# Seven of sixteen experts on slots of 64 tokens, in plain fp32 on two column tiles of TensorE

## What is computed

```python
scores = sigmoid(h @ w_router)
sel = scores + b_router
...  # best of 4 groups of 4 experts, then the top 2 experts in it
combine = sum(one_hot(idx, 16) * wts[..., None], axis=1)
for e in range(16):
    y_e = (silu(h @ w1[e]) * (h @ w3[e])) @ w2[e]      # 1024 -> 512 -> 1024
    y = y + combine[:, e:e + 1] * y_e
```

## Time and profile before

| | |
|---|---|
| median of 3 runs | 941.02 us |
| lowest and highest | 938.82, 943.4 us |
| the profiled execution: span from first to last instruction | 937.8 us |
| TensorE, VectorE, ScalarE, POOL busy over the span | 88%, 67%, 55%, 24% |
| read from HBM, written | 190.64 MB, 23.10 MB |
| granted TensorE clock, mean | 0.960 of full |

### The profile page before, as it was taken

One profiled execution on the slowest core, in us unless ns is written; L12 is line 12 of the kernel. 1 busy time (PEld: TensorE's weight loads), 2 busy tenths in 40 slices (PEclk: granted clock), 3 DMA queues, 4 the chain that ended last, 5 costly groups with the idle time before them and its releaser, 6 DMA issues. The chain is left out here.

```text
span 937.8 us, 15876 instructions
## 1 busy us (share of the span) xinstructions
PE 822.2 (88%) x6374; PEld 696.5 (74%) x6374; DVE 625.2 (67%) x804; ACT 515.8 (55%) x814; POOL 222.9 (24%) x336
## 2 busy tenths in 40 slices
PE   4998997999889998798769789849999999999990
PEld 2677866889669886598659788737888888888870
DVE  1596764458553685345455457487999998999965
ACT  3575742457424663237433344357877777777751
POOL 3114161123301252013400110016232222321112
PEclk9999999999989999899989999959999999999996
DMA  9977468245862369437685238807999999999934
GB/s 313 280 244 191 123 167 214 67 111 143 183 178 80 102 155 228 104 84 257 192 200 169 83 116 289 329 10 254 344 363 385 380 378 383 388 373 374 380 144 156
DMA packets 220053, 209.00 MB, mean 223 GB/s; under 512 B 51101, under 2 KB 156230, under 8 KB 219338
## 3 DMA queue, kind: packets, MB, share of 16 engines
q1 hardware_dynamic: 217241, 203.80, 68.9%
q0 software_dynamic: 2736, 4.15, 1.3%
HBM read 190.64 MB, written 23.10 MB: 228 GB/s over the span
## 5 line engine op out<-in xcount | busy, mean ns | idle before, releaser
L2061 DVE TENSOR_TENSOR w_lo<-raw,w_hi 128x2048 fp32r<-128x2048 f32 x96 | 233.4, 2450 | 23.1 <-ACT w_hi L1496 22.1
L2282 PE MATMUL bank<-hT,half_hi 128*128 128x256 f32 (+1 forms) x1024 | 229.8, 320 | 11.5 <-DVE half_lo L1616 5.3
L1496 ACT CAST w_hi<-raw 128x2048 fp32r<-128x2048 f32 x96 | 183.2, 1912 | 41.1 <-PE bank L2282 39.5
L2282 PEld LDWEIGHTS bank<-hT,half_hi 128*128 128x128 f32 x1024 | 168.3, 194 | 27.8 <-issue 9.3
L2282 PE MATMUL bank<-hT,half_lo 128*128 128x256 f32 (+1 forms) x512 | 160.2, 313 | 0.0
L2282 PE MATMUL bank<-w_hi,window 128*128 128x512 f32 x480 | 156.8, 398 | 0.0
L1616 DVE TENSOR_TENSOR half_lo<-half_raw,half_hi 128x1024 fp32r<-128x1024 f32 x88 | 108.7, 1237 | 55.5 <-ACT half_hi L1056 55.0
L2282 PE MATMUL bank<-lane 64*64 64x64 f32 (+2 forms) x2096 | 101.9, 237 | 19.4 <-issue 8.0
L2282 PEld LDWEIGHTS bank<-lane 64*64 64x64 f32 (+2 forms) x2096 | 93.4, 149 | 30.9 <-issue 15.6
L1056 ACT CAST half_hi<-half_raw 128x1024 fp32r<-128x1024 f32 x88 | 92.1, 1048 | 25.7 <-PE bank L2282 9.2
L2282 PEld LDWEIGHTS bank<-w_hi,window 128*128 128x128 f32 x480 | 90.4, 188 | 20.5
(11 more groups left out here) (321 smaller groups left out, 1272.3 us busy)
## 6 DMA issues: line engine op xcount, KB each, us to landing
raw<-in_w_e_dram SPq DMA_DIRECT2D x96, 1024.0 KB, 8.6
half_raw<-in_w_in_dram SPq DMA_DIRECT2D x64, 512.0 KB, 5.1
half_raw<-in_w_ada_dram SPq DMA_DIRECT2D x32, 512.0 KB, 4.9
raw<-in_w_ada_dram SPq DMA_DIRECT2D x8, 1024.0 KB, 11.3
dense<-staged SPq DMA_DIRECT2D x32, 128.0 KB, 4.5
half_raw<-in_w_proj_a_dram SPq DMA_DIRECT2D x8, 512.0 KB, 5.4
half_raw<-in_w_proj_b_dram SPq DMA_DIRECT2D x8, 512.0 KB, 4.1
half_raw<-in_w_out_dram SPq DMA_DIRECT2D x8, 512.0 KB, 8.0
```

The source lines that it names most:

```text
L1496: act.copy(e_hi[n % WBUF][:, :], slots[n % SLOTS_AHEAD][:, :]).then_inc(s["hi_ready"], 1)
L2061: dve.tensor_tensor(e_lo[n % WBUF][:, :], slots[n % SLOTS_AHEAD][:, :], e_hi[n % WBUF][:, :].bitcast(F32), ALU.subtract)\
L2282: return nc.tensor.matmul(dst, lhsT, rhs, start=start, stop=stop)
```

## The change

**Ranking.** Experts 0 and 1 stay in their places. The other fourteen are ranked on the chip by their number of tokens (`rank_loads`, `order_experts` on VectorE), and places 2 to 15 of the stream take them in a fixed pattern: ranks 1 to 7 go to wide places of 128 rows, ranks 8 to 14 to narrow places of 64. There are 512 rows, so rank 8 has at most 512 / 8 = 64. The pattern is `WIDTH`: places 0, 1, 3, 5, 7, 9, 11, 13 and 14 are wide, places 2, 4, 6, 8, 10, 12 and 15 narrow. SP reads an expert's number from `order_int` into a register before its first load.

**Narrow experts.** Their weights are not split: the product is plain fp32, straight from the slot of the ring, so the slot is freed by TensorE (`unit_used`) and not by VectorE. The window is hi + lo, [128, 8, 64]. The output has 64 rows, so the array is used as two tiles of 64 columns: in `narrow_up` the tiles take the two halves of a chunk's 512 columns, in `narrow_down` the two halves of the output's 1024, with both down units at once. Activations are [128, 256], turned in two pieces and copied once (`narrow_act`); the output needs one copy (`narrow_copy`) in place of two.

**Bookkeeping.** POOL's set-up writes the tables for it (some 30 small operations more). `place_rows` counts the expert of the last place, and not number 15, as the last. The last place's store is two DMAs of 64 rows. All 96 units are still loaded.

```diff
+FIXED = 2
+RANKED = EXPERTS - FIXED
+WIDTH = [WIDE, WIDE] + 6 * [NARROW, WIDE] + [WIDE, NARROW]
...
+        SPLIT_UNITS = [n for n, (_, q, _) in enumerate(STREAM) if WIDTH[q] == WIDE]
+        def wide_ahead(q):
+            first = UP_FIRST[q] + WBUF
+            down = [n for n in (first, first + 1) if q and n in SPLIT_UNITS]
+            up = [n for n in range(UP_FIRST[q + 1] if q + 1 < EXPERTS else len(STREAM), len(STREAM))[:4] if n in SPLIT_UNITS]
+            return down, up
...
             for n, (v, q, half_) in enumerate(STREAM):
-                if n >= SLOTS_AHEAD:
-                    sp.wait_ge(s["unit_split"], n - SLOTS_AHEAD + 1)
+                if n == UP_FIRST[FIXED]:
+                    sp.wait_ge(s["routing_ready"], 2)
+                if q == len(expert):
+                    expert.append(sp.value_load(order_int[0:1, q:q + 1], min_val=FIXED, max_val=EXPERTS - 1))
+                before = n - SLOTS_AHEAD
+                if before >= 0 and before in SPLIT_UNITS:
+                    sp.wait_ge(s["unit_split"], SPLIT_UNITS.index(before) + 1)
+                elif before >= 0:
+                    sp.wait_ge(s["unit_used"], before + 1)
...
-            last_rows = slice(LISTED, FIRST_TURN)
+            sp.wait_ge(s["y_copied"], 2 * EXPERTS)
             for nh in range(2):
-                sp.wait_ge(s["y_copied"], 2 * (EXPERTS - 1) + nh + 1)
-                sp.dma_start(y_dram[last_rows, nh * N:nh * N + N], y_out[1][:, nh * N:nh * N + N]).then_inc(s["stored"], 16)
+                sp.dma_start(y_dram[LISTED:FIRST_TURN, nh * N:nh * N + N], y_out[1][NARROW * nh:NARROW * nh + NARROW, 0:N])\
+                    .then_inc(s["stored"], 16)
...
             for q in range(EXPERTS):
-                first = UP_FIRST[q] + WBUF
-                ahead = [n for n in range(first, first + (6 if q else 4)) if n < len(STREAM)]
-                for n in ahead[:1]:
+                down, up = wide_ahead(q)
+                for n in down[:1]:
                     expert_high(n)
-                if q:
+                if q and WIDTH[q - 1] == WIDE:
                     act_high(q - 1)
...
+            def narrow_up(q, m):
+                dst = work_bank(q, m)
+                if m == 0:
+                    pe.wait_ge(s["window_ready"], q)
+                    pe.wait_ge(s["act_split"], q - 1)
+                for kh in range(2):
+                    weights = unit_landed(UP_FIRST[q] + 2 * m + kh)
+                    for kc in range(4):
+                        c = 4 * kh + kc
+                        for half in range(2):
+                            ins = mm(dst[NARROW * half:NARROW * half + NARROW, 0:256], narrow_window[q % 2][:, c, :],
+                                     weights[:, kc, 256 * half:256 * half + 256], c == 0, c == KC - 1)
+                    ins.then_inc(s["unit_used"], 1)
...
+            def narrow_down(q):
+                pe.wait_ge(s["act_split"], q + 1)
+                pe.wait_ge(s["y_copied"], 2 * (q - 2) + 2)
+                weights = [unit_landed(DOWN_FIRST[q] + nh) for nh in range(2)]
+                for c in range(4):
+                    half = c // 2
+                    for nh in range(2):
+                        ins = mm(work_bank(q, 2)[NARROW * nh:NARROW * nh + NARROW, :],
+                                 act_narrow[:, c % 2, NARROW * half:NARROW * half + NARROW], weights[nh][:, c, :], c == 0, c == 3)
+                        if c == 3:
+                            ins.then_inc(s["unit_used"], 1)
```

More of the change, by code:

```diff
@@ L48 @@
 LISTED = 512
-FIRST_TURN = LISTED + 128
+FIRST_TURN = LISTED + 64
 SKIPPED = 4096
 HALF_BLOCK = 64
+WIDE, NARROW = P, P // 2
+FIXED = 2
+RANKED = EXPERTS - FIXED
+WIDTH = [WIDE, WIDE] + 6 * [NARROW, WIDE] + [WIDE, NARROW]
+RANK_AT = [WIDTH[FIXED:q + 1].count(WIDE) if WIDTH[q] == WIDE else WIDTH[FIXED:].count(WIDE) + WIDTH[FIXED:q + 1].count(NARROW)
+           for q in range(FIXED, EXPERTS)]
+assert all(TOP * SEQ // r <= NARROW for r, w in zip(RANK_AT, WIDTH[FIXED:]) if w == NARROW) and WIDTH[-1] == NARROW
 COL_U, COL_V, COL_Q, COL_K, COL_VV, COL_Z = 0, D, 2 * D, 3 * D, 4 * D, 5 * D
@@ L539, in four @@
             return t[:, :].rearrange("p (c n) -> p c n", c=4)
+        SPLIT_UNITS = [n for n, (_, q, _) in enumerate(STREAM) if WIDTH[q] == WIDE]
+        SPLIT_TOTAL = len(SPLIT_UNITS)
+        WIDE_BEFORE = [WIDTH[:q].count(WIDE) for q in range(EXPERTS + 1)]
+        LAST_NARROW = TOP * SEQ - NARROW
+        def wide_ahead(q):
[3 more added lines that the diff above has]
+            return down, up
         def chunk_at(pos, d):
@@ L1534, in y_copy, with narrow_copy @@
                 act.copy(y_out[q % 2][:, nh * N:nh * N + N], work_bank(q, 2 + nh)[:, :]).then_inc(s["y_copied"], 1)
+            def narrow_copy(q):
+                act.wait_ge(s["unit_used"], DOWN_FIRST[q] + 2)
+                if q >= 2:
+                    act.wait_ge(y_stored[q % 2], 16 * (q // 2))
+                act.copy(y_out[q % 2][:, 0:N], work_bank(q, 2)[:, :]).then_inc(s["y_copied"], 2)
             for c in range(KC):
@@ L1586, in _ @@
             with act.If(act.value_load(overflow_int[0:1, 0:1], min_val=0, max_val=1) > 0):
+                act.wait_ge(s["unit_used"], ALL_UNITS)
                 act.wait_ge(s["stored"], 32)
@@ L2217, in _ @@
             for q in range(EXPERTS):
-                first = UP_FIRST[q] + WBUF
-                ahead = [n for n in range(first, first + (6 if q else 4)) if n < len(STREAM)]
-                for n in ahead[:1]:
+                down, up = wide_ahead(q)
+                for n in down[:1]:
                     expert_low(n)
-                if q:
+                if q and WIDTH[q - 1] == WIDE:
                     act_low(q - 1)
-                for n in ahead[1:3]:
+                elif q:
+                    narrow_act(q - 1)
+                for n in down[1:]:
+                    expert_low(n)
+                early = 2 if q == 0 else 1 if WIDTH[q] == WIDE else 0
+                for n in up[:early]:
                     expert_low(n)
                 act_product(q)
-                for n in ahead[3:]:
+                for n in up[early:]:
                     expert_low(n)
@@ L2953, in down_half, with unit_landed @@
                 ins.then_inc(s["unit_used"], 1)
+            def unit_landed(n):
+                pe.wait_ge(landed[n % SLOTS_AHEAD], 16 * fills_until(n))
+                return four(slots[n % SLOTS_AHEAD])
+            def narrow_up(q, m):
[11 more added lines that the diff above has]
+                    ins.then_inc(s["unit_used"], 1)
@@ new lines, in narrow_turn @@
+            def narrow_turn(q):
+                pe.wait_ge(s["act_done"], q + 1)
+                for c in range(2):
+                    ins = turn(work_bank(q, 0)[:, c * P:(c + 1) * P], act_nat[:, c * P:(c + 1) * P])
+                ins.then_inc(s["act_turned"], 1)
+            def narrow_down(q):
[9 more added lines that the diff above has]
+                            ins.then_inc(s["unit_used"], 1)
@@ L2955, in _, with turn_of, down_of @@
+            def turn_of(q):
+                if WIDTH[q] == WIDE:
+                    turn_act(q)
+                else:
+                    narrow_turn(q)
+            def down_of(q):
+                if WIDTH[q] == WIDE:
+                    down_half(q, 0)
+                    down_half(q, 1)
+                else:
+                    narrow_down(q)
             for q in range(EXPERTS):
-                up_half(q, 0)
+                up = up_half if WIDTH[q] == WIDE else narrow_up
+                up(q, 0)
```

208 lines of the change are left out of this document (150 added, 58 removed).

## The result

The changed kernel takes 957.67 us (median of 4, 955.57 to 960.43) against 942.21 for the kernel before (four runs; the 941.02 that the forecast started from is the median of the first three): ratio 1.0177, 95% interval 1.0135 to 1.0219. It is 1.8% **slower**; forecast were 934.9 us and a range of 926 to 949. A second, later series gave 952.91 us and 1.0112 (1.0077 to 1.0147), which is told with the experiments. Every ratio here is of fast executions alone; this leaves out one of 4509 us of the kernel before in e1, and one of 949.7 us of it beside e5 to e8. The profiled execution has a span of 955.0 us against 937.8.

The account below looks back on a forecast made before the run. TensorE was taken to bound the experts' stage narrowly, the change moving the bound to the transfers. Last landing 3.2 us later, less 9.3 gained in the tail, is -6.1 on 941.0: 934.9 us, range 926 to 949.

Parts of the forecast that it names:

- What bounds it: Sixteen experts' stage: TensorE leads narrowly and may get 2 to 5% faster before transfers bound it, at 2.81 us a unit.
- Price of a narrow expert: On TensorE: 11.5 us in place of 17.17, with up units at 1.85 us, down pair 3.7, tiles overlapping.
- The early part: First narrow expert's units keep their slots until TensorE has used them, so unit 19 lands 0.5 us later.
- The middle: Units 19 to 95: 213.6 us of transfers plus 2.5 us for five handovers; unit 95 lands 3.2 us later.
- the margin of 0.7 us: Ring of five slots: fifth unit on, due at 16.9 us, lands at the earliest at 16.2, so no loss.
- The rival that had the clock fall at every handover: Middle: low clock delays slot release, five times 13.5 us in place of 2.5; 945.9 to 949.7 us; chance 0.25.
- Its deciding point: Handovers: the clock case holds once the slot comes free later than 11.9 us after the last wide landing.
- The tail: After unit 95's landing: the first rows decide, 18.3 us in place of 27.6, so 9.3 us gained.
- What costs nothing: POOL's set-up (some 5 us), VectorE's ranking (0.7 us uncovered, hidden by TensorE) and SP's register loads add nothing.
- The time: Whole kernel: 3.2 us later landing less 9.3 us in the tail, -6.1 on the 941.0 median, 934.9 us.

Follow-up runs that it names:

- e1: The kernel before, unchanged, run and profiled a second time: 940.99 us against 941.21, ratio 0.9989.
- e5: The changed kernel, unchanged, run and profiled a second time: 952.91 us, ratio 1.0112 to the kernel before.
- e8: Changed kernel with only the last expert narrow, but slots of experts 2, 4, ... 12 given back after TensorE's use: 952.17 us, ratio 1.0149.
- e11: Changed kernel with its seven narrow experts in one run at the end, plus 16 unread products ahead of narrow down pairs: 939.13 us, ratio 0.9983.
- e6: Changed kernel with the narrow down pair one unit earlier and 12 unread products in TensorE's gap: 941.50 us, ratio 1.0005.
- e2: Changed kernel with one narrow expert alone, the last: 942.56 us, ratio 1.0015.
- e3: Changed kernel with 20 unread products after each narrow expert's up units: 948.91 us, ratio 1.0090.
- e9: The kernel before plus the changed kernel's POOL set-up operations, written to tiles nobody reads: ratio 1.0019.
- e4: Changed kernel with a narrow expert's down pair multiplied one unit earlier: 945.99 us, ratio 1.0059.
- e12: Repeat of e11, the same kernel: 936.42 us, ratio 0.9973.

## Why the prediction was wrong

**What bounds it: half right.** A landing follows the one before by 2.71 us when nothing stands between. e11's narrow experts came 16.66 us apart at 384 GB/s, of which 6 x 2.71 = 16.26 are units; if the other 0.40 is the store of a narrow expert's rows, half the size of a wide one's, a wide expert is 17.06 by transfers, against TensorE's 17.17. By this estimate the slack was under 1%, not "2 to 5%". The price of 2.81 us a unit for the changed kernel, two experts in 33.7 us, agrees with it (17.06 + 16.66), but no run shows it for experts in turns: the lowest there is 34.37 (e6).

**Price of a narrow expert: right.** A narrow up unit takes 1.73 to 1.8 us for 1.85, a down pair 3.6 for 3.7. The tiles overlap.

**The early part: small miss.** Unit 19 came 1.6 us later by column B, not 0.5. Unit 15 was issued 27.1 us after A as forecast, but landed 5.4 us later, not 5.0, and units 16 to 19 took 11.8 us more for the 11.2 of the sum. All five profiles with this order of experts have 44.2 to 45.4 in column B, and those with no narrow expert so early and no late release 41.2 to 42.9, so the narrow expert makes it. VectorE's ordering of the experts, 0.7 us by the prediction, is this block, first and last rows of it in the changed kernel's timeline:

```profile
649.54 1.86 DVE L2263 COPY ordered<-counted 128x4 f32<-128x4 f32 x1
651.33 0.16 DVE L2265 COPY ordered<-holder 128x14 f32<-128x14 f32 x1
...
653.47 0.18 DVE L2274 CAST first_int<-ordered 128x16 int32<-128x16 f32 x1
653.68 0.17 DVE L2275 CAST order_int<-load_rank 128x14 int32<-128x14 f32 x1
```

It is 4.3 us from 649.54, in a stage where VectorE has hardly any idle time. e2, which up to its last experts differs from before only by the routing part and the loads' register reads, has TensorE 1.7 us later at unit 49 (141.7 us after its first unit, before 140.0); its column B is that of before all the same.

**The middle: the step that failed.** The forecast put the loss at the handovers at 2.5 us, "half" of the clock's, with the argument that a late TensorE also shortens the next gap by as much. It does not. The gap ends when units issued at the end of the narrow down pair have landed and are split, so all of it moves along with a late TensorE, and nothing is won back: the five gaps kept 5.90 to 7.14 us, in e5 5.90 to 6.79, and the clock fell at each of the ten. C grew by 12.8 and 15.8 us.

The forecast's second fault is the margin of 0.7 us that it gave the pair's release. In its own terms the loop is 5.0 us to the first landing, 2.8 to the next, 4.4 for the split, 17.1 for six wide units with their transposes and 3.7 for the pair: 33.0 us, 0.7 under the transfers' 33.7. Measured at the first handover were 6.1, 3.0, 4.9, 18.7 and 3.6. The landing after a release took 5.4 to 6.2 us in all five, not "the shortest time seen", and the activation's split, 0.7 us, is queued on VectorE ahead of the first product. Without the 2.0 us of low clock this loop would by estimate still be 34.4 us, the pace of the kernel before; e3's four periods with the clock up, 34.4 to 35.0, agree.

The rival that had the clock fall at every handover was given 0.25 and priced at 13.5 us, near the 12.8 and 15.8. Its mechanism was right, its price in part luck: it counted two low stretches a turn, 3.4 us, where there was one, 2.0 us, and the longer landings made up the rest. Its deciding point, a release over 11.9 us after the last wide landing, did not decide: the first was 11.4, the others 12.4 to 14.7, and the periods were all long.

**The tail: sized wrong.** 5.3 us were gained after the last landing, not 9.3. The down pair ended at T + 6.2 as forecast, T being the landing of unit 95, 923.20. But unit 95 had landed at 900.6 before, not at 898.0 (the DMA share of a window was taken for a landing), so 25.0 us were to be beaten, not 27.6: 2.6 of the 4.0 us. The first rows do decide, as forecast, and are later, in the changed kernel's timeline:

```profile
925.02 0.58 ACT L1611 COPY y_out<-bank 128x512 f32<-128x512 f32 x1 [2.17 <-PE bank L2415]
...
926.40 0.96 POOL L1066 DMA_INDIRECT expert_rows<-y_out,store_int  x1 [15.36 <-ACT y_out L1611]
...
931.30 0.99 POOL L1022 DMA_INDIRECT y_tok<-expert_rows,row_int  x1 [3.94 <-issue]
...
938.15 2.48 DVE L2395 SCALAR_TENSOR_TENSOR y_tok<-y_tok,pair_weight,ada_vec 128x1024 f32<-128x1024 f32 x2 [12.48 <-DMA y_tok<-expert_rows,row_int]
940.67 2.29 DVE L2400 TENSOR_TENSOR arena_hi<-arena_hi,y_tok 128x2048 f32<-128x2048 f32 x1
```

The store takes 4.9 us where the earlier trace rows have 3.5, the gather 6.85 for 7.6; the second rows are added from 942.88 on, T + 19.7 for 18.3.

**What costs nothing.** POOL's set-up costs nothing that can be told (e9). VectorE's ordering is not nothing (above).

**The time.** With the clock rival the sum was 945.9 to 949.7. The second series, 952.9, is 3 us beyond it, and the tail alone was 4.0 us short. The first, 957.7, is 4.8 us above the second; its profile has column A 4.1 us later, of which the prediction could know nothing, since it had one profile. That this holds for the whole series is not shown.

## What to carry to other kernels

When a consumer takes over the release of a buffer from a faster one, draw the loop from its release through issue, landing, conversion and work back to its next release, and compare its length with the period: what lies on such a loop is paid in full every turn, a low clock too, and nothing catches up. Order the work so that what holds slots is used first (one unit earlier took the ratio from 1.0112 to 1.0059, some 5 us), and put unlike tiles in one run, not in turns (0.9996). Before an engine is relieved, ask how far the next bound is; here it was under 1% away, by the estimate above.

## What was not expected of the hardware

- Two executions of one program run the same products at 26 to 32 us at full and at half pace (1.05 and 1.87 us for the same eight), while the granted clock's row says 1.00 in both: a product's own duration is the better witness. Ahead of the experts this and the like made 641.8 to 644.2 us in two profiles of one kernel, 645.9 to 650.0 in two of the other.
- Between A and the tail the granted clock fell after every idle gap of TensorE of 3.0 us or more, in all profiles here, and after none of 1.6 us or less. In between it went either way: after 1.89, 1.90 and 2.45 us it fell (e6), after 2.22 and 2.60 it did not (e4). Of one kernel, the changed one, the product behind a gap of 2.72 us at 918.08 took 0.79 us (e5), and that behind 2.74 us at 919.20 took 0.51 (first profile). Products that nobody reads brought 3 to 7 us (e3) and 5 to 6 us (e11, e12) from column B to D.
- A copy of four elements a partition took 1.86 us on VectorE, between operations of 0.16 to 0.56. The record shows more than its length: POOL's copy of a window is under way, and VectorE's ends 0.02 to 0.03 us after it in all eleven profiles that have both. In the changed kernel POOL's is

```profile
648.49 2.89 POOL L1030 CAST window<-hT 128x2048 fp32r x1 [24.06 <-issue]
```

which ends at 651.38, and VectorE's, from 649.54, at 651.41. So it looks like a wait of one engine for the other, some 1.7 us of the 4.3 of the ordering; moving POOL's copy was not tried.
